# A block ahead of the barrier, evictions with the norm's factor, and head-norm matmuls between pairs of k tiles in a two-layer hybrid decoder step

## The chip, the cores and the metric

The kernel runs on one core of a Trainium2 chip. The time is device time of one execution in microseconds (us), lower is better. Before the change it is 3043.86 us, the median of three runs (3041.05 to 3045.55).

## The reference

One step of a two-layer decoder for 256 prompt tokens and 8 sample tokens (264 columns), all in fp32. Per layer:

```
xn = rmsnorm(x, norm_mix);  proj = xn @ w_in        # 2048 -> u, q, k, v, qi, ki, wi, gates
q = rope(rmsnorm(q, q_norm)); k = rope(rmsnorm(k, k_norm)); qi, ki = rope(qi), rope(ki)
y_att = sparse attention: an indexer (qi, ki, wi) picks keys (top 64 prompt, top 256 sample)
y_ssm = S5 scan of u (state 64 groups x 64), gelu, gated by w_glu
x = x + (sig(g0) * (y_ssm @ w_branch0) + sig(g1) * (y_att @ w_branch1)) @ w_out
x = x + (silu(hn @ w_gate) * (hn @ w_up)) @ w_down,  hn = rmsnorm(x, norm_ffn)
```

The outputs are x, the new keys, values and indexer keys of each layer, and the last states of the scan. `rmsnorm(x, g)` is x times g times one factor per token, 1/sqrt(mean(x^2) + eps); the head norm is the same over the 128 entries of a head.

## The kernel before

Activations lie transposed: 128 features on the partitions, the 264 tokens as columns; x has 16 such slices (k tiles). Weights stream through a ring of six slots of 512 KB, one *unit* (128 outputs, 8 k tiles) in each; two units make a block f (units 2f and 2f+1) and one output slice. SyncE loads unit u once unit u-6 is done (semaphore `units`). A block accumulates in one of four PSUM banks (`main[f % 4]`), and whoever evicts it frees the bank (`bank_free`).

A matmul is either *plain* (fp32, raw weights; each shows as two records) or *split*: ScalarE casts the weights to their high part (L1051, `highs_to`), VectorE subtracts to get the low part (L1355, `lows_to`), the activations are split likewise (x_high by ScalarE at L1088, x_low by VectorE at L1362), and three one-pass matmuls (L624, L625, L626) replace one plain product (L628). Units 2 to 9 (blocks 1 to 4) are plain; from unit 10 on they are split, apart from some later ones. `SPLIT` lists them, and TensorE waits before each split unit for its low part. All engines run their streams in the order written.

**Start of a layer.** The layers are separated by a barrier of all engines; ahead of the first one stands a prologue that loads x, squares it, and scales it by the gains (xg). After it, in each layer, TensorE sums the squares over the partitions with a matmul by ones (L655); ScalarE takes the root (L1082), VectorE the reciprocal (L1358), and makes the 16 slices xn = xg times factor (L1365), then the 16 x_low. Blocks 1 and 2 take xg, so that their results are multiplied by the factor as VectorE evicts them (L1370); blocks 3 and 4 take xn and ScalarE evicts them (L1061). VectorE then makes the S5 angles (L1376 to L1390), a chain of 15 small operations (L1394 to L1408), three wide ones (L1413 to L1415), the lows of units 10 and 11, three wide ones (L1417 to L1419), the lows of units 12 and 13, powers (L1431 to L1436), the lows of units 14 and 15. ScalarE has an Exp (L1090), which needs a table load, right after the x_high.

In layer 0 the end of the FFN's last phase makes xg for layer 1 (L1847) and adds the squares (L1856), and SyncE loads units 2 to 7 of layer 1 at L543.

**Head norm.** ScalarE squares a head slice (L1179, two buffers), TensorE adds it over its partitions into row t of one bank (L817: weights 128 rows by 12 columns) for 12 heads; ScalarE takes the root (L1193), VectorE the reciprocal (L1645), and TensorE spreads row t over 128 partitions (L833: weights 12 rows by 128 columns) into one of four banks, from which VectorE scales the head (L1653). Between these stand `fill(n)`, n whole w_in units of 24 split matmuls: unit 93 after the first `spread_rows` (L808, part of the sample key selection, 128x128), 94 after the second, 95 after head sum 8, 96 and 97 after the last sum, 98 after spread 5 and 99 after the last. Then follows `s5_out(0)` (L769). `LATE` gives which of four places holds the high part of units 92 to 105; places 2 and 3 lie on data of the key selection, so ScalarE waits for its end (`gix_ready`) before it writes them.

**End.** x is stored in four parts of four slices (528 KB), each when its last slice is final (L571).

Of the kernel before, what the change touches and what calls it, by code (L numbers as in the profile page):

```python
# [51 lines left out]
LATE = {92: 0, 93: 1, 94: 0, 95: 1, 96: 2, 97: 3, 98: 0, 99: 2, 100: 3, 101: 0, 102: 2, 103: 3, 104: 0, 105: 2}  # L52
# [64 lines left out]
def build(nc, d, o):  # L117
    with ExitStack() as ctx:
# [295 lines left out]
        qroped = sem("qroped")  # L414
        vt_ready, v_copied, kvn_ready, kvn_copied = sem("vt_ready"), sem("v_copied"), sem("kvn_ready"), sem("kvn_copied")
# [25 lines left out]

        with nc.Block() as block:
            @block.sync
            def _(sp):
                for p in range(4):
                    sp.dma_start(x[:, 4 * p:4 * p + 4, :], d["x"][:, 4 * p:4 * p + 4, :]).then_inc(x_part[p], 16)
                sp.dma_start(consts[:, 0:4 * P], d["consts"][:, 0:4 * P]).then_inc(consts_in, 16)
                for u in range(2, 4):
                    sp.dma_start(ring[:, u, :], d["w_in"][0, u - 2]).then_inc(u_in[u], 16)
                sp.dma_start(consts[:, 4 * P:NCONST], d["consts"][:, 4 * P:NCONST]).then_inc(consts_rest, 16)  # L450
                for u in range(4, 8):
                    sp.dma_start(ring[:, u % 6, :], d["w_in"][0, u - 2]).then_inc(u_in[u % 6], 16)

            @block.scalar
            def _(act):
                act.dma_start(gn[:], d["gn"][0]).then_inc(gn_in, 16)
                act.dma_start(tables, d["tables"]).then_inc(tables_in, 16)
                for p in range(4):
                    act.wait_ge(x_part[p], 16)
                    nc.scalar.activation(first_sq[:, 4 * p:4 * p + 4, :], x[:, 4 * p:4 * p + 4, :], ACT.Square).then_inc(sq_ready, 1)  # L460
                    if p >= 2:
                        act.wait_ge(gn_in, 16)
                        for k in range(4 + 2 * p, 6 + 2 * p):
                            nc.scalar.activation(xg[:, k, :], x[:, k, :], ACT.Copy, scale=gn[:, 0, k:k + 1])

                act.wait_ge(sq_ready, 4)
                nc.scalar.activation(small[:, 6:7], first_sq[:, 0, 0:1], ACT.Sqrt)

            @block.vector
            def _(dve):  # L470
                v = nc.vector
                tt, tsc = v.tensor_tensor, v.tensor_scalar
                v.memset(small[:, 7:8], EPS)

                def add_part(p):
                    dve.wait_ge(sq_ready, p + 1)
                    if p >= 2:
                        dve.wait_ge(sq_added, p - 1)
                    tt(acc, first_sq[:, 0:4, :] if p == 1 else acc, first_sq[:, 4 * p:4 * p + 4, :], ALU.add).then_inc(sq_added, 1)

                dve.wait_ge(gn_in, 16)
                for p in (0, 1, 3):
                    dve.wait_ge(x_part[p], 16)
                    for k in range(4 * p, 4 * p + 4):
                        tsc(xg[:, k, :], x[:, k, :], gn[:, 0, k:k + 1], None, ALU.mult)
# [28 lines left out]
        for layer in range(DEPTH):  # L514
            with nc.Block() as block:
# [11 lines left out]
                def _(sp):  # L527
# [45 lines left out]
                    for up, count, cols, half, n0, _ in PHASES:  # L573
# [8 lines left out]
                        if not up and half == 1:  # L582
# [14 lines left out]
                    if layer == DEPTH - 1:  # L597
                        sp.wait_ge(x_out, 64 * DEPTH)
# [3 lines left out]
                def _(pe):  # L602
                    mm = nc.tensor.matmul

                    def unit_part(u, seq, c, full, high, low, k0, n, opens, closes, made=None):
# [23 lines left out]
                        if k0 + n == 8:  # L629
                            m.then_inc(units, 1)  # L630
# [4 lines left out]
                    def w_in_unit(f, c, made=None):  # L635
                        unit_part(2 * f + c, f, c, xg if f < 3 else xn, xh, xl, 0, 8, c == 0, c == 1, made)
# [10 lines left out]
                    def x_made(k):  # L647
                        pe.wait_ge(xn_ready, k + 1)

# [153 lines left out]
                    def spread_rows(h):  # L803
# [6 lines left out]
                        fill(1)  # L810

                    def sum_heads(first, last):
                        for t in range(first, last + 1):
                            if t == 0:
# [3 lines left out]
                               start=t == 0, stop=t == NHK - 1).then_inc(qsum_ready, 1)  # L818

# [3 lines left out]
                    sum_heads(6, 8)  # L823
                    fill(1)
                    sum_heads(9, NHK - 1)
                    fill(2)
                    pe.wait_ge(spread_used, 6)
                    for t in range(NHK):
# [6 lines left out]
                        if t in (5, NHK - 1):  # L835
                            fill(1)
# [184 lines left out]
                    for up, count, cols, half, n0, seq0 in PHASES:  # L1021
                        if up:
                            split_blocks(seq0, n0, 2 * HF, 2, 8, xfh, xfl, None if half else x_scaled)
                        else:
                            split_blocks(seq0, n0, NT, 2, 11, hdh, hdl, hidden(half))

                @block.scalar
                def _(act):
# [67 lines left out]
                    for f in range(3, 10):  # L1096
                        evac_one(f)
                    act.drain()
                    act.wait_ge(bank_free[1], 4)
                    act.wait_ge(bank_free[2], 3)  # L1100
# [73 lines left out]
                    for t in range(NHK):  # L1174
# [10 lines left out]
                        if t == 10:  # L1185
                            act.wait_ge(gix_ready, 1)
                            highs_to(96)
                        if t == 11:
                            highs_to(97)
                            evac_gates(47, 1)  # L1190
# [3 lines left out]
                    highs_to(98)  # L1194
# [143 lines left out]
                def _(dve):  # L1338
# [25 lines left out]
                    for k in range(NT):  # L1364
                        tt(xn[:, k, :], xg[:, k, :], rs[:, 0, :], ALU.mult).then_inc(xn_ready, 1)  # L1365
                    for k in range(NT):
                        split_low(k)
                    for f in range(1, 3):
                        dve.wait_ge(units, 2 * f + 2)
                        tt(proj[:, f, :], main[f][:, 0:T], rs[:, 0, :], ALU.mult).then_inc(bank_free[f], 1)  # L1370
# [20 lines left out]
                    lows_to(8)  # L1391
# [147 lines left out]
                    def pick():  # L1539
# [24 lines left out]
                        lows_to(93)  # L1564
                        for h in range(2):
                            if h == 1:
                                lows_to(94)
# [12 lines left out]
                        lows_to(97)  # L1580
# [66 lines left out]
                    lows_to(98)  # L1647
                    for t in range(12):
                        if t == 6:
                            lows_to(99)  # L1650
# [163 lines left out]
                    def finish(i, s, up, half, n0, seq0):  # L1814
# [22 lines left out]
                        if not up and s % 2 == 1:  # L1837
# [7 lines left out]
                            if half == 1 and layer < DEPTH - 1:  # L1845
                                k = 4 * i + m
                                tsc(xg[:, k, :], x[:, k, :], gn[:, 0, k:k + 1], None, ALU.mult)  # L1847
# [217 lines left out]
```

## Time and profile before

| | us |
|---|---|
| median of three runs | 3043.86 |
| profiled execution | 3041.63 |
| its span | 3039.8 |
| VectorE busy in the span | 1965.2 (65%) |
| ScalarE busy | 1247.8 (41%) |
| first matmul of layer 0 | 14.81 after the span's start |
| last matmul before layer 1's barrier ends | 1522.12 |
| last VectorE operation of the program ends | 3035.62 |
| first of x loads issued in the prologue | 0.74 |

The profile names engines PE (TensorE), PEld (its weight loads), DVE (VectorE), ACT (ScalarE), POOL (GpSimd) and SP (SyncE). A share of busy time is an average; what a change is worth is read at the place where TensorE waits. Ends of matmuls are modelled, so paces are taken from one start to the next.

### The profile page before, as it was taken

Reading aid. Unit: us, or ns where it says so; the run is one execution under the profiler, and the core shown is the slowest. Engines: PE = TensorE matmul, PEld = TensorE weight load, DVE = VectorE, ACT = ScalarE, POOL = GpSimd, SP = SyncE. Lnnn points to the kernel's source line nnn. Section 1 sums busy time; section 2 is a strip of 40 time slices with the busy share of each in tenths; the row PEclk is TensorE's granted clock in tenths of the full one; section 3 lists DMA queues with packets and bytes.
Section 4 is the critical chain, followed back from the end, with each engine's and each line's share of the span. In section 5 each row is a group of like instructions: output and inputs, shape, how many; then the busy total and the mean of one; then the engine's idle time right before and its main releaser. Section 6 shows DMA issues by size and latency. Waiting matters only on the chain. (4 is left out here: it accounts for less than half of the span.)

```text
span 3039.8 us, 58606 instructions
## 1 busy us (share of the span) xinstructions
PE 2994.0 (98%) x23480; PEld 2852.2 (94%) x23480; DVE 1965.2 (65%) x3141; ACT 1247.8 (41%) x1767; POOL 253.3 (8%) x239
## 2 busy tenths in 40 slices
PE   8999999999999999999999999999999999999999
PEld 7988888999999999999988888889999999999999
DVE  7559888577655545555575697885776565455653
ACT  4443333544554333334344422344445443333332
POOL 4320000400000000000043200013000000000000
PEclk9999999999999999999999999999999999999999
DMA  7547444745655655556555473447556555555564
GB/s 253 164 145 203 145 141 145 243 167 178 196 185 182 199 172 174 185 181 206 187 194 167 149 204 126 143 163 230 170 177 199 182 183 198 167 181 181 185 205 135
DMA packets 150191, 546.45 MB, mean 180 GB/s; under 512 B 19824, under 2 KB 25072, under 8 KB 149520
## 3 DMA queue, kind: packets, MB, share of 16 engines
q1 hardware_dynamic: 137296, 507.40, 50.0%
q0 software_dynamic: 12096, 35.67, 4.6%
q8 instruction: 112, 1.84, 0.3%
q10 hardware_dynamic: 640, 1.16, 0.1%
q14 instruction: 47, 0.39, 0.0%
HBM read 536.95 MB, written 7.21 MB: 179 GB/s over the span
## 5 line engine op out<-in xcount | busy, mean ns | idle before, releaser
L1790 DVE TENSOR_TENSOR w_ffn_low<-ring_ffn,w_ffn_high 128x1024 fp32r<-128x1024 f32 (+1 forms) x480 | 638.8, 1332 | 456.0 <-ACT w_ffn_high L1300 456.0
L1300 ACT ACTIVATE w_ffn_high<-ring_ffn 128x1024 fp32r<-128x1024 f32 (+1 forms) x480 | 547.9, 1142 | 641.8 <-PE main L1013 640.9
L1011 PE MATMUL main<-x_ffn_high,w_ffn_high 128*128 128x264 f32 x2816 | 792.1, 281 | 0.0
L1013 PE MATMUL main<-x_ffn_high,w_ffn_low 128*128 128x264 f32 x2816 | 791.7, 281 | 0.0
L1012 PE MATMUL main<-x_ffn_low,w_ffn_high 128*128 128x264 f32 x2816 | 791.7, 281 | 0.0
L1011 PEld LDWEIGHTS main<-x_ffn_high,w_ffn_high 128*128 128x128 f32 x2816 | 526.8, 187 | 0.1
L1012 PEld LDWEIGHTS main<-x_ffn_low,w_ffn_high 128*128 128x128 f32 x2816 | 526.8, 187 | 0.1
L1013 PEld LDWEIGHTS main<-x_ffn_high,w_ffn_low 128*128 128x128 f32 x2816 | 526.8, 187 | 0.0
L1013 PE MATMUL main<-hidden_high,w_ffn_low 128*128 128x264 f32 x1408 | 395.8, 281 | 0.0
L1011 PE MATMUL main<-hidden_high,w_ffn_high 128*128 128x264 f32 x1408 | 395.8, 281 | 0.0
L1012 PE MATMUL main<-hidden_low,w_ffn_high 128*128 128x264 f32 x1408 | 395.8, 281 | 0.0
L628 PE MATMUL main<-xn,ring 128*128 128x264 f32 x1632 | 377.6, 388 | 0.0
L628 PEld LDWEIGHTS main<-xn,ring 128*128 128x128 f32 x1632 | 305.4, 190 | 49.9 <-issue 0.8
L626 PE MATMUL main<-x_high,w_low 128*128 128x264 f32 x1200 | 342.0, 285 | 0.0
L1011 PEld LDWEIGHTS main<-hidden_high,w_ffn_high 128*128 128x128 f32 x1408 | 263.4, 187 | 0.0
L1012 PEld LDWEIGHTS main<-hidden_low,w_ffn_high 128*128 128x128 f32 x1408 | 263.4, 187 | 0.0
L1013 PEld LDWEIGHTS main<-hidden_high,w_ffn_low 128*128 128x128 f32 x1408 | 263.4, 187 | 0.0
L624 PE MATMUL main<-x_high,w_in_high 128*128 128x264 f32 x880 | 259.4, 295 | 3.4 <-DVE w_low L1355 3.1
L625 PE MATMUL main<-x_low,w_in_high 128*128 128x264 f32 x880 | 250.1, 284 | 0.0
L626 PEld LDWEIGHTS main<-x_high,w_low 128*128 128x128 f32 x1200 | 227.4, 190 | 0.0
L1051 ACT ACTIVATE w_mid_high<-ring 128x1024 fp32r<-128x1024 f32 x144 | 151.5, 1055 | 144.4 <-PE main L626 144.4
L1355 DVE TENSOR_TENSOR w_low<-ring,w_mid_high 128x1024 fp32r<-128x1024 f32 x144 | 175.5, 1224 | 52.8 <-ACT w_mid_high L1051 51.1
(373 smaller groups left out, 4767.7 us busy)
## 6 DMA issues: line engine op xcount, KB each, us to landing
ring_ffn<-in_w_up SPq DMA_DIRECT2D x352, 512.0 KB, 3.2
ring<-in_w_in SPq DMA_DIRECT2D x260, 512.0 KB, 3.4
ring_ffn<-in_w_down SPq DMA_DIRECT2D x128, 704.0 KB, 4.1
ring<-in_w_br SPq DMA_DIRECT2D x64, 512.0 KB, 3.9
ring<-in_w_out SPq DMA_DIRECT2D x64, 512.0 KB, 3.1
w_low<-in_w_in POOLq DMA_DIRECT2D x20, 512.0 KB, 6.9
ring<-in_w_glu SPq DMA_DIRECT2D x16, 512.0 KB, 3.7
out_x<-x SPq DMA_DIRECT2D x8, 528.0 KB, 5.9
```

The source lines that it names most:

```text
L624: mm(out, weight(wh, u, k), high[:, kk, :], start=starts, stop=False)
L625: mm(out, weight(wh, u, k), low[:, kk, :], start=False, stop=False)
L626: m = mm(out, weight(wl, u, k), high[:, kk, :], start=False, stop=stops)
L628: m = mm(out, weight(raw, u, k), full[:, kk, :], start=starts, stop=stops)
L1011: mm(out, wfh[:, slot, w], high[:, kk, :], start=kk == 0, stop=False)
L1012: mm(out, wfh[:, slot, w], low[:, kk, :], start=False, stop=False)
L1013: m = mm(out, wfl[:, slot, w], high[:, kk, :], start=False, stop=kk == chunks * kts - 1)
L1051: af(high, raw, ACT.Copy).then_inc(unit_high, 1)
L1300: af(wfh[:, s, 0:cols], ring_ffn[:, s, 0:cols], ACT.Copy).then_inc(high_ready, 1)
L1355: tt(low, raw, high.bitcast(F32), ALU.subtract).then_inc(unit_low, 1)
L1790: tt(wfl[:, s, 0:cols], ring_ffn[:, s, 0:cols], wfh[:, s, 0:cols].bitcast(F32), ALU.subtract).then_inc(low_ready, 1)
```

## The change

1. Block 2 (units 4 and 5) is computed ahead of the barrier, from xg: in the prologue for layer 0, at the end of layer 0 for layer 1 (`first_block`). Its weights are loaded ahead of the other units. After the barrier TensorE does L655, block 1, then 3 and 4. `units` is raised by three when unit 3 is done.
2. Blocks 3 and 4 take xg too, and VectorE evicts all four with the factor (`gather_block`). The xn and x_low operations alternate. The casts of units 10 and 11 move ahead of ScalarE's Exp, the lows of both behind the angles.
3. Each of the 12 head sums and 12 spreads is followed by two k tiles of w_in (6 split matmuls, `pair`), with one whole unit between sums and spreads. `LATE` and the places of casts and lows of units 94 to 99 follow.
4. At the end of layer 1, slices 12 to 15 of x are stored one by one.

```diff
+        def first_block(pe, layer, gained):
+            for u in (4, 5):
+                pe.wait_ge(u_in[u], 16 * (G_END // 6 * layer + 1))
+                for k in range(8):
+                    kk = 8 * (u - 4) + k
+                    gained(kk)
+                    nc.tensor.matmul(main[2][:, 0:T], ring[:, u, k * P:(k + 1) * P], xg[:, kk, :], start=kk == 0, stop=kk == NT - 1)
@@ prologue, sync: x parts 0, 1, unit 4, x parts 2, 3, consts, units 5, 2, 3, consts, units 6, 7
+            @block.tensor
+            def _(pe):
+                def gained(k):
+                    if 8 <= k < 12:
+                        pe.wait_ge(x_gained_act, k - 7)
+                    else:
+                        pe.wait_ge(x_gained, k + 1 if k < 8 else k - 3)
+                first_block(pe, 0, gained)
@@ layer, sync, end
-                                for u in range(2, 8):
+                                for u in (4, 5, 2, 3, 6, 7):
                                     prefetch(u)
-                            store_x(3)
+                            if layer < DEPTH - 1:
+                                store_x(3)
+                                continue
+                            for k in range(12, NT):
+                                sp.wait_ge(resid, 2 * NT + k + 1)
+                                sp.dma_start(o["x"][:, k, :], x[:, k, :]).then_inc(x_out, 16)
@@ layer, tensor
-                            m.then_inc(units, 1)
+                            m.then_inc(units, 3 if u == 3 else 1)
-                        unit_part(2 * f + c, f, c, xg if f < 3 else xn, ...)
+                        unit_part(2 * f + c, f, c, xg if f < 5 else xn, ...)
-                    w_in_blocks(1, 2)
-                    for c in range(2):
-                        w_in_unit(3, c, x_made)
-                    w_in_blocks(4, 1)
+                    w_in_blocks(1, 1)
+                    w_in_blocks(3, 2)
@@ head norm, tensor
-                        fill(1)
+                    def pair(n):
+                        nonlocal filled
+                        w_in_piece(filled // 2, filled % 2 * 8 + n % 4 * 2, 2)
+                        filled += n % 4 == 3
@@ in sum_heads, after the matmul of head t
+                            pair(t)
                     spread_rows(0)
                     sum_heads(0, 5)
                     spread_rows(1)
-                    sum_heads(6, 8)
+                    sum_heads(6, NHK - 1)
                     fill(1)
-                    sum_heads(9, NHK - 1)
-                    fill(2)
@@ in the spreads, after the matmul of head t
-                        if t in (5, NHK - 1):
-                            fill(1)
+                        pair(t)
@@ layer 0, tensor, after the last FFN phase
+                    if layer < DEPTH - 1:
+                        pe.wait_ge(bank_free[2], (SEQ_UP + 4 * HF + 2 * NT) // 4 + 1)
+                        first_block(pe, layer + 1, lambda k: pe.wait_ge(x_gained, k + 1))
@@ scalar
                         af(xh[:, k, :], xn[:, k, :], ACT.Copy).then_inc(xh_ready, 1)
+                    highs_to(11)
                     act.wait_ge(params_in, 80)
                     af(disc[:, 0, :], ssmp[:, 2, :], ACT.Exp).then_inc(trig_ready, 1)
@@ vector, start of a layer
+                    def gather_block(f):
                         dve.wait_ge(units, 2 * f + 2)
-                        tt(proj[:, f, :], main[f][:, 0:T], rs[:, 0, :], ALU.mult).then_inc(bank_free[f], 1)
+                        tt(proj[:, f, :], main[f % 4][:, 0:T], rs[:, 0, :], ALU.mult).then_inc(bank_free[f % 4], 1)
+                    for k in range(NT + 2):
+                        if k < NT:
+                            tt(xn[:, k, :], xg[:, k, :], rs[:, 0, :], ALU.mult).then_inc(xn_ready, 1)
+                        if k >= 2:
+                            split_low(k - 2)
+                    for f in range(1, 4):
+                        gather_block(f)
@@ vector, after the angles
-                    lows_to(8)
+                    lows_to(11)
+                    gather_block(4)
                     dve.wait_ge(trig_ready, 4)
```

## Rows read from the trace of the kernel before

**Rows 1.** The page: busy time, share, count of each engine.
```profile
PE 2994.0 (98%) x23480; PEld 2852.2 (94%) x23480; DVE 1965.2 (65%) x3141; ACT 1247.8 (41%) x1767; POOL 253.3 (8%) x239
```

**Rows 2.** Timeline of TensorE at layer starts: start, length, instruction, count [idle before, releaser].
```profile
46.25 0.48 PE L624 MATMUL main<-x_high,w_in_high 128*128 128x264 f32 x1
...
1525.53 1.22 PE L655 MATMUL side<-rs,consts 128*128 128x264 f32 x2 [3.41 <-PEq L1943]
...
1555.96 0.48 PE L624 MATMUL main<-x_high,w_in_high 128*128 128x264 f32 x1
```

**Rows 3.** Busy time by stage: PE, PEld, DVE, ACT, POOL; PEclk, DMA, GB/s.
```profile
14.80:20.00 5.20, 5.19 (x12) 4.07 (x13) 3.39 (x6) 1.60 (x5) 0.07 (x1) 1.00 1.05 392
20.20:32.00 11.80, 11.80 (x55) 10.08 (x54) 9.66 (x29) 5.78 (x15) 8.91 (x2) 1.00 0.58 202
1887.20:1890.60 3.40, 3.40 (x18) 3.40 (x17) 1.01 (x1) 0.00 (x0) 0.00 (x0) 0.50 0.00 0
```

**Rows 4.** Timeline of VectorE across the start of layer 1.
```profile
1523.02 0.96 DVE L1856 TENSOR_TENSOR rs<-rs,tmp 128x264 f32<-128x264 f32 x2
...
1529.14 5.59 DVE L1365 TENSOR_TENSOR xn<-arena,rs 128x264 f32<-128x264 f32 x16
...
1542.12 0.43 DVE L1370 TENSOR_TENSOR proj<-main,rs 128x264 f32<-128x264 f32 x1 [1.54 <-PE main L628]
...
1545.02 0.19 DVE L1394 TENSOR_TENSOR apow<-proj 128x32 f32<-128x32 f32 x1 [0.41 <-ACT proj L1095]
...
1552.22 2.36 DVE L1355 TENSOR_TENSOR w_low<-ring,w_in_high 128x1024 fp32r<-128x1024 f32 x2
...
1558.37 2.40 DVE L1355 TENSOR_TENSOR w_low<-ring,w_in_high 128x1024 fp32r<-128x1024 f32 x2
...
1565.56 2.36 DVE L1355 TENSOR_TENSOR w_low<-ring,w_in_high 128x1024 fp32r<-128x1024 f32 x2
```

**Rows 5.** Timeline of ScalarE at the start of layer 1.
```profile
1535.20 1.28 ACT L1090 ACT_TABLE_LOAD   x1
...
1544.90 1.04 ACT L1051 ACTIVATE w_in_high<-ring 128x1024 fp32r<-128x1024 f32 x1
```

**Rows 6.** Timeline of TensorE where the kind of matmul changes, layer 0.
```profile
101.31 1.05 PE L682 MATMUL side<-proj,consts 128*128 128x264 f32 x4
...
102.32 0.28 PE L625 MATMUL main<-x_low,w_in_high 128*128 128x264 f32 x1
...
361.12 0.28 PE L626 MATMUL main<-x_high,w_low 128*128 128x264 f32 x1
361.32 1.74 PE L817 MATMUL side<-tmp,rs 128*12 128x264 f32 x6
363.00 0.39 PE L624 MATMUL main<-x_high,w_in_high_v 128*128 128x264 f32 x1
363.22 0.28 PE L625 MATMUL main<-x_low,w_in_high_v 128*128 128x264 f32 x1
...
373.83 2.93 PE L833 MATMUL side<-rs,consts 12*128 12x264 f32 x12
376.70 0.39 PE L624 MATMUL main<-x_high,w_in_high_b 128*128 128x264 f32 x1
```

**Rows 7.** DMA issues: the first 4 us (ring), and the last store; KB each, us to landing.
```profile
ring<-in_w_in SPq DMA_DIRECT2D x2, 512.0 KB, 8.1
...
out_x<-x SPq DMA_DIRECT2D x1, 528.0 KB, 2.7
```

**Rows 8.** Timelines of TensorE and VectorE in the head norm's stretch.
```profile
348.47 1.91 PE L808 MATMUL side<-proj 128*128 128x390 f32 x6
...
385.77 3.84 PE L769 MATMUL side<-arena,cc 128*32 128x264 f32 x64
...
1866.24 2.02 PE L808 MATMUL side<-proj 128*128 128x390 f32 x6
...
1870.84 1.23 DVE L1355 TENSOR_TENSOR w_low<-ring,w_in_high_v 128x1024 fp32r<-128x1024 f32 x1
```

More of the change, by code:

```diff
@@ L414, in build @@
         qroped = sem("qroped")
+        x_gained, x_gained_act = sem("x_gained"), sem("x_gained_by_act")
         vt_ready, v_copied, kvn_ready, kvn_copied = sem("vt_ready"), sem("v_copied"), sem("kvn_ready"), sem("kvn_copied")
@@ L444, in _, with load_x, load @@
             def _(sp):
-                for p in range(4):
+                def load_x(p):
                     sp.dma_start(x[:, 4 * p:4 * p + 4, :], d["x"][:, 4 * p:4 * p + 4, :]).then_inc(x_part[p], 16)
+                def load(u):
+                    sp.dma_start(ring[:, u % 6, :], d["w_in"][0, u - 2]).then_inc(u_in[u % 6], 16)
+                load_x(0)
+                load_x(1)
+                load(4)
+                load_x(2)
+                load_x(3)
                 sp.dma_start(consts[:, 0:4 * P], d["consts"][:, 0:4 * P]).then_inc(consts_in, 16)
-                for u in range(2, 4):
-                    sp.dma_start(ring[:, u, :], d["w_in"][0, u - 2]).then_inc(u_in[u], 16)
+                for u in (5, 2, 3):
+                    load(u)
                 sp.dma_start(consts[:, 4 * P:NCONST], d["consts"][:, 4 * P:NCONST]).then_inc(consts_rest, 16)
-                for u in range(4, 8):
-                    sp.dma_start(ring[:, u % 6, :], d["w_in"][0, u - 2]).then_inc(u_in[u % 6], 16)
+                for u in (6, 7):
+                    load(u)
+            @block.tensor
[6 more added lines that the diff above has]
+                first_block(pe, 0, gained)
             @block.scalar
@@ L597, in _ @@
                     if layer == DEPTH - 1:
-                        sp.wait_ge(x_out, 64 * DEPTH)
+                        sp.wait_ge(x_out, 64 * DEPTH + 48)
                     sp.wait_ge(stored, 48)
@@ L635, in w_in_unit @@
                     def w_in_unit(f, c, made=None):
-                        unit_part(2 * f + c, f, c, xg if f < 3 else xn, xh, xl, 0, 8, c == 0, c == 1, made)
+                        unit_part(2 * f + c, f, c, xg if f < 5 else xn, xh, xl, 0, 8, c == 0, c == 1, made)
                     def w_in_blocks(first, count):
@@ L1095, in _ @@
                     af(disc[:, 5, :], disc[:, 6, :], ACT.Sin).then_inc(trig_ready, 1)
-                    for f in range(3, 10):
+                    for f in range(5, 10):
                         evac_one(f)
                     act.drain()
-                    act.wait_ge(bank_free[1], 4)
-                    act.wait_ge(bank_free[2], 3)
+                    for bank in range(4):
+                        act.wait_ge(bank_free[bank], 4 if bank < 2 else 3)
                     act.sem_inc(proj_copied, 10)
@@ L1193, in _ @@
                     af(rs[0:NHK, 0, :], side[0][0:NHK, 0:T], ACT.Sqrt, bias=small[0:NHK, 7:8], scale=1.0 / HD).then_inc(qstd_ready, 1)
-                    highs_to(98)
+                    highs_to(97)
+                    evac_gates(47, 1)
+                    act.wait_ge(gix_ready, 1)
                     highs_to(99)
@@ L1579, in pick @@
                         dve.sem_inc(gix_ready, 1)
-                        lows_to(97)
+                        lows_to(96)
                     def scan(half, between=None):
@@ L1645, in _ @@
                     v.reciprocal(rs[0:NHK, 0, :], rs[0:NHK, 0, :]).then_inc(qinv_ready, 1)
-                    lows_to(98)
+                    lows_to(97)
                     for t in range(12):
-                        if t == 6:
-                            lows_to(99)
+                        if t in (2, 6):
+                            lows_to(98 + t // 6)
                         dve.wait_ge(qinv_spread, t + 1)
```

25 lines of the change are left out of this document (6 added, 19 removed).

## The prediction

> **What bounds the kernel now.** I read the page's busy times first: TensorE is busy for 98% of the span [rows 1]. So only three things move the time: its remaining idle, work whose pace is below the full one, and anything new that keeps it waiting. The waits view gives 18.2 us of TensorE's idle to the two layer starts (14.8 and 3.4), and about 1 us at a time elsewhere. The timeline of TensorE then shows where each layer's first split block starts [rows 2]; the table by stage shows its pace [rows 3]; the timelines of VectorE and ScalarE show who feeds it there [rows 4, 5]; and the single rows around the small matmuls show what a change from one kind of matmul to another costs [rows 6].
>
> Paces that I use. A plain fp32 product is two records of 0.222 us at full speed (55 records touch 11.8 us), so a w_in block of 16 products takes 7.1 us; at the start of the run the step is 0.44 (12 records in 5.2 us) although that stretch's granted clock is noted as 1.00, and TensorE had been idle before it [rows 3]. A split k tile is three records of about 0.121, so a pair of k tiles is 0.73 us, a unit 2.9 and a block 5.9.
>
> **Part 1, the block ahead and the four evictions with the norm's factor.** Call L the start of the matmul at L655, the first work of a layer. The new block now stands ahead of the barrier, so the barrier waits for it. In layer 1 its weights are issued at 1510 and its last input is scaled at 1523.1, just after the last FFN matmul ends (1525.53 less 3.41 idle is 1522.1) [rows 2]. It runs 1522.1 to 1529.3. Before, VectorE's last add ended at 1523.98 and L655 came 1.55 us later [rows 2, 4]; with that same distance L becomes 1530.8, 5.3 later than 1525.53. In layer 0 the unit of weights that stood sixth, after 2.4 MB, landed 8.1 us after its issue at 3.4, thus at 11.5 [rows 7]; at the implied 1.3 us for each transfer, the one that now stands third (the block's first unit) lands at about 7.4, and the one that stands seventh (its second unit) where the seventh landed before, 8.1 after 3.9: 12.0. TensorE starts at 7.4 with 12 records at 0.44, then 20 at 0.222: it ends at 17.1, L is 18.7 instead of 14.8. If it is at full speed sooner, the second unit's landing still bounds it: 12.0 plus 3.6 plus 1.5 is 17.1.
>
> From L on TensorE has L655 and three plain blocks (0.5 and 21.4): block 5, the first split one, can start at L+21.9 and end at L+27.7. Before it started at 46.25 and 1555.96 [rows 2], so by TensorE alone 5.7 and 3.3 us would be won.
>
> VectorE's chain hangs on L, and it is nearly gapless already: its idle between 1529 and 1559 is 1.54 and 0.41 [rows 4]. Step by step: the factor is there and xn begins at L+3.0 (1525.53 to 1529.14, less 0.6 that L655 lost to the slow clock); 32 operations of xn and x_low, now alternating, 11.2: L+14.2. Three evictions of 0.44, the third not before its block ends at L+14.7: L+15.6. ScalarE has its sixteenth x_high at about L+14.0; then, new and ahead of the Exp, the two casts of units 10 and 11 at 1.04 each, then the table load of 1.28 [rows 5]: Exp ends at L+17.7. Before, this load lay under x_low; now VectorE waits about 2 us for it. Its angle operations (1542.55 to 1544.6) end at L+19.9, the lows of units 10 and 11 at L+22.2, in time for block 5. Then the fourth eviction, 0.4; then what the change leaves between lows 11 and 12: the chain from 1545.02 to 1552.22, 7.2, which used to stand ahead of low 10, and three wide operations, 3.8; low 12 ends at L+34.8. Block 5 ends at L+27.7. **TensorE waits 7 us for low 12 in each layer.** Block 6 then starts at 53.5 instead of 52.1, and at 1565.6 instead of 1561.8. Low 14 comes 7.2 after low 12 (1558.37 to 1565.56) [rows 4] while block 6 lasts 5.9, another 1.3; the slow clock that a 7 us stop should bring costs about the same and lies beside this wait, 0.1 more. Layer 0 loses 2.8, layer 1 loses 5.2: **8.0**. Units 16 on find VectorE caught up. The weight loads of units 10 and 11 are issued at L+7.6 together with 9 and are back before ScalarE's casts at L+14; sample keys on GpSimd's queue are asked for no later. Bounds: layer 0 from -0.1 (L at 17.1) to +3.5, layer 1 from +3.7 (no low 14 wait) to +6.
>
> **Part 2, the head norm's sums and spreads.** The rows show three cases [rows 6]. A group with 128 rows and 128 columns, L682, costs nothing extra: from its first record to the second of the following split is 1.01, that is 4 times 0.222 and 0.12. L817, 128 rows by 12 columns: 0.20 from the last split record to it instead of 0.12; its six records take 1.68 instead of 1.34; and the first step of the split after it is 0.22 instead of 0.12. L833, 12 rows by 128 columns and no square to wait for: its 12 records take 2.87 instead of 2.67; with the same 0.09 ahead and 0.10 behind, a round trip costs 0.39. Of L817's 0.34 in the middle I give 0.11 to the way out, as half of L833's 0.20, and 0.23 to the one wait for ScalarE's square that falls among three heads (two buffers): a round trip costs 0.30. I take 0.30 and 0.39, since they are the same instructions on both sides of the passage; the other end is L682's nothing.
>
> The Trainium skill, TensorEngine Tiling (Array Packing), section Key Properties, says that changing the tiling mode, not just the tile, drains the engine; TensorE: Matmul & The Clock Gate gives a drain as some 0.175 us. By that estimate two passages cost 0.35 per head; the sum would be 0.1 us higher. It is a rule against this change, and these rows bear it out, L682's exemption too.
>
> Before, a layer made 5 such round trips; changed, it makes 24. The changed stretch from the first L808 to L769: two groups L808 at 1.6 (1.91 with the last record's modelled end), 12 heads at 0.445+0.73+0.30=1.47, one unit 2.9, 12 spreads at 0.445+0.73+0.39=1.56: 42.4. New in it is a wait: low 95 stands behind two groups of the second spread on VectorE, ending 5.9 after that L808 begins (1866.24 to 1870.84 and 1.23) [rows 8], while the pair of head 8 wants it at 5.1: 0.7. So 43.1 against 385.77-348.47=37.3 in layer 0 [rows 8]: +5.8. In layer 1 two stretches of 3.4 us at half clock follow the two L833 groups (one shown) [rows 3]; the units in them take 1.5 longer each, which alternating work should spare: 43.1 against 40.4, +2.7. Together **+8.5**. The square waits are in this. ScalarE's root and VectorE's reciprocal lie beside the one unit between sums and spreads (2.9, with the root no longer behind a Tanh eviction); without that cover 0.5 each. Bounds: no passage cost, 24 heads at 1.17, is 34.1, plus a longer low 95 wait 1.4: -1.8 and -4.9; above, both spreads partly at half clock, +5.
>
> **Part 3, last slices singly.** The last store moves 132 KB instead of 528 KB, of a landing of 2.7 [rows 7]; at the same rate of some 400 KB per us 1.0 less. The three earlier singles lie under the last matmuls; the last wait counts all. -1.0, bounds -1.3 and 0.
>
> Sum: 8.0+8.5-1.0=+15.5. The profiled execution took 3041.6, thus 3057.1; the three timed runs have a median 2.2 higher, and against 3043.9 it is 3059.4. I say 3059. What the measurement can tell from no change is about 0.2%, 6 us.
>
> **The rivals.**
> - B, passages are free when a head stands alone between pairs, its weights loaded under the split matmuls that run. For it: L682 [rows 6]. Against: both odd shapes pay on both sides. (The Trainium skill, TensorE: Matmul & The Clock Gate, section Part 2, has weight loads pulled ahead of matmuls in flight; that alone would give this 3044.) Heads -6.7 in all, total +0.3: 3044, no change. It decides by one price: at 48 round trips the kernel is slower by over 0.2% from about 0.13 each, and not slower below 0.01.
> - C, VectorE keeps up at the layer starts, since alternating xn with x_low frees ScalarE earlier. Then the 5.7 and 3.3 are won: -9.0+8.5-1.0, 3042. Against: the 12.6 us on VectorE between lows 11 and 12 are in program order, against 5.9 of block 5.
> - D, B and C both: 3027.
> - E, the alternating stretches hold TensorE at half clock at times, as after the L833 groups before. For it: 12-row work half the time. A third of the two spread stretches at half speed costs some 6: 3065.
>
> Chances: forecast 0.60, B 0.13, C 0.10, D 0.04, E 0.13. The forecast and E are slower, with a small part of B and C: slower 0.76; same 0.16; faster 0.08. Range 3043 to 3066: it holds half of C and most of B, and the upper bounds short of their sum.
>
> **What would show it.** In the changed profile: the 16 products of the block end at about 17 and 1529, L655 starts at about 18.7 and 1530.8; TensorE's waits name the low of w_in (L1355's successor) with about 7 us before block 6 in each layer and 1 before block 7; one step of a pair loop is 1.47 (sums) and 1.56 (spreads); the stretch from first L808 to L769 is 43 in both layers, with no half clock in layer 1. The prediction is wrong if low 12 comes before L+28, or if the pair loop steps at 1.2.

## The result, and the profile after

The changed kernel takes 3060.5 us (median of 5 runs, 3059.8 to 3061.2), the kernel before 3044.8 beside it (5 runs, 3041.1 to 3045.6): a ratio of 1.0056, interval 1.0046 to 1.0067, or 15.7 us slower. The forecast was 3059. A second comparison on another chip gave the same: 3060.1 against 3043.9, 1.0056 (1.0043 to 1.007). Of all executions of the kernels below one stands apart: one of the 12 of e3_full took 5113.1 us, at a mean granted clock of 0.643, and its ratio leaves it out.

The page first. It hardly tells the two kernels apart: TensorE has as many instructions as in [rows 1] and 11.6 us more busy time. A *passage* is the change from one shape of matmul to another, on the way in or out. Work that passages or a slow clock stretch counts as busy; only the rest of the 19.6 us by which the span grew, 8.0, is idle.

```profile
PE 3005.6 (98%) x23480; PEld 2850.8 (93%) x23480; DVE 1967.2 (64%) x3145; ACT 1249.0 (41%) x1763; POOL 247.5 (8%) x239
```

Next the view of waits for TensorE, which says what it waited for: us in total, times, longest.

```profile
PE main L658 <- DVE w_low L1388: 19.6, 9, 7.7
PE main L450 <- DVE arena L514: 7.5, 1, 7.5
...
PE side L957 <- DMA bbt<-in_ck,gix: 2.7, 2, 1.7
PE side L686 <- PEq L1979: 1.5, 1, 1.5
PE side L686 <- PEq L541: 1.5, 1, 1.5
```

The lows of w_in (L1388, before L1355) lead it, with 7.7 as the longest. Where that falls stands in TensorE's timeline; its rows answer to [rows 2]. L450 is the block ahead, L686 was L655, L658 was L624.

```profile
7.51 8.96 PE L450 MATMUL main<-arena,ring 128*128 128x264 f32 x32 [7.51 <-DVE arena L514]
18.01 0.69 PE L686 MATMUL side<-rs,consts 128*128 128x264 f32 x2 [1.54 <-PEq L541]
...
39.70 0.48 PE L658 MATMUL main<-x_high,w_in_high 128*128 128x264 f32 x1
52.97 0.56 PE L658 MATMUL main<-x_high,w_in_high 128*128 128x264 f32 x1 [7.08 <-DVE w_low L1388]
61.37 0.28 PE L658 MATMUL main<-x_high,w_in_high 128*128 128x264 f32 x1
...
1531.78 7.28 PE L450 MATMUL main<-arena,ring 128*128 128x264 f32 x32
1540.60 0.68 PE L686 MATMUL side<-rs,consts 128*128 128x264 f32 x2 [1.54 <-PEq L1979]
...
1562.94 0.36 PE L658 MATMUL main<-x_high,w_in_high 128*128 128x264 f32 x1 [0.30 <-issue]
1576.69 0.56 PE L658 MATMUL main<-x_high,w_in_high 128*128 128x264 f32 x1 [7.67 <-DVE w_low L1388]
```

The reader is to see block 5 start 6.5 us sooner than before in layer 0 (39.70 against 46.25), and block 6 then stand still for 7.1 and 7.7 us. Block 7 starts at 61.37, so block 6 lasted 8.4 us where a block at full speed lasts 5.8. The windows say why, and give the head norm's stretches (first L837, which was L808, to first L798, which was L769). Columns as in [rows 3]; the figure behind the five busy times, 0.51 in the first row, is the granted clock.

```profile
48.50:58.70 10.20, 5.73 (x27) 5.76 (x28) 9.40 (x23) 0.02 (x1) 0.00 (x0) 0.51 0.05 17
1574.20:1581.00 6.80, 4.31 (x20) 4.34 (x21) 6.21 (x17) 0.00 (x0) 0.00 (x0) 0.51 0.00 0
351.79:395.21 43.42, 43.06 (x231) 28.50 (x229) 24.57 (x45) 15.40 (x24) 0.00 (x0) 1.00 0.26 85
1874.86:1918.28 43.42, 43.05 (x231) 28.50 (x229) 24.55 (x45) 15.40 (x24) 0.00 (x0) 1.00 0.26 85
```

The head norm's stretches of the kernel before, the same view:

```profile
348.47:385.77 37.30, 37.03 (x230) 28.70 (x228) 25.14 (x45) 14.94 (x24) 0.00 (x0) 1.00 0.30 99
1858.24:1898.61 40.37, 40.10 (x231) 31.77 (x229) 25.15 (x45) 14.94 (x24) 0.00 (x0) 0.92 0.28 92
```

During the stop the granted clock falls to one half (1.2 GHz instead of 2.4) and stays there into block 6. The head norm takes 43.4 us in both layers, with no slow clock in it, against 37.3 and 40.4 before. One step of its sums, in TensorE's timeline (answers to [rows 6]; a step is from one L850 to the next: 1.47):

```profile
353.64 0.62 PE L850 MATMUL side<-tmp,rs 128*12 128x264 f32 x2
...
355.11 0.62 PE L850 MATMUL side<-tmp,rs 128*12 128x264 f32 x2
...
356.58 0.62 PE L850 MATMUL side<-tmp,rs 128*12 128x264 f32 x2
```

VectorE in layer 1 (answers to [rows 4]): the wait for the Exp behind the casts, lows 10 and 11, the fourth eviction L1399, the chain from L1432, and only then lows 12 and 13.

```profile
1559.41 0.19 DVE L1413 TENSOR_TENSOR proj<-proj 128x32 f32<-128x32 f32 x1 [3.42 <-ACT proj L1125]
...
1561.62 2.35 DVE L1388 TENSOR_TENSOR w_low<-ring,w_in_high 128x1024 fp32r<-128x1024 f32 x2
1563.89 0.42 DVE L1399 TENSOR_TENSOR proj<-main,rs 128x264 f32<-128x264 f32 x1
1564.23 0.18 DVE L1432 TENSOR_TENSOR apow<-proj 128x32 f32<-128x32 f32 x1
...
1575.32 2.36 DVE L1388 TENSOR_TENSOR w_low<-ring,w_in_high 128x1024 fp32r<-128x1024 f32 x2
```

ScalarE there (answers to [rows 5]): both casts waited for their weights, 0.63 and 0.43 us.

```profile
1554.81 1.06 ACT L1085 ACTIVATE w_in_high<-ring 128x1024 fp32r<-128x1024 f32 x1 [0.63 <-DMA ring<-in_w_in]
...
1556.30 1.06 ACT L1085 ACTIVATE w_in_high<-ring 128x1024 fp32r<-128x1024 f32 x1 [0.43 <-DMA ring<-in_w_in]
```

And the last store (answers to [rows 7]), 132 KB, landed 1.8 us after its issue instead of 2.7:

```profile
out_x<-x SPq DMA_DIRECT2D x1, 132.0 KB, 1.8
```

Between the two profiled executions the time went to: layer starts +3.3 (the transposes L700 at 78.85 against 75.58) and +6.8 (1601.96 against 1585.31 is 16.7, less the 9.8 gathered by the end of layer 0); head norm +6.1 and +3.0; tail -0.9; that is 18.3 of the 19.6 by which the span grew. The remaining 1.3 are about what the longer wait for the key gather makes: 2.7 above, and in TensorE's waits of before

```profile
PE side L926 <- DMA bbt<-in_ck,gix: 1.3, 2, 0.8
```

The medians differ by less, 15.7, because the profiled execution of before was one of its fastest. The mean granted clock of each execution shows what sets them apart. Of the 38 of before on the two chips used last below, those with a clock of 0.998, as the profiled one had, took 3040.7 to 3043.5 us, and those with 0.996 or 0.997 took 3043.6 to 3046.0. So the kernel before loses more to half clock in most of its executions than its trace shows.

### The profile page after: what moved, and what is told of

Its sections match the earlier page's. It is cut to its first block and busy times, and to the rows that moved or that the text cites. A ratio compares the mean times of both kernels' runs of the same rounds, so it can differ in the third digit from the quotient of the medians.

```text
span 3059.4 us, 58609 instructions
## 1 busy us (share of the span) xinstructions
PE 3005.6 (98%) x23480; PEld 2850.8 (93%) x23480; DVE 1967.2 (64%) x3145; ACT 1249.0 (41%) x1763; POOL 247.5 (8%) x239
## 5 line engine op out<-in xcount | busy, mean ns | idle before, releaser
L662 PE MATMUL main<-xn,ring 128*128 128x264 f32 x1504 | 348.8, 388 | 0.0
L662 PEld LDWEIGHTS main<-xn,ring 128*128 128x128 f32 x1504 | 280.9, 190 | 45.9 <-issue 0.8
L658 PE MATMUL main<-x_high,w_in_high 128*128 128x264 f32 x880 | 261.5, 297 | 18.4 <-DVE w_low L1388 17.9
L1388 DVE TENSOR_TENSOR w_low<-ring,w_mid_high 128x1024 fp32r<-128x1024 f32 x144 | 175.6, 1225 | 52.6 <-ACT w_mid_high L1085 50.9
```

Of the source, the lines that this page charges most:

```text
L658: mm(out, weight(wh, u, k), high[:, kk, :], start=starts, stop=False)
L662: m = mm(out, weight(raw, u, k), full[:, kk, :], start=starts, stop=stops)
L1388: tt(low, raw, high.bitcast(F32), ALU.subtract).then_inc(unit_low, 1)
```

## The experiments

All times are medians, each ratio is to the kernel before on the same chip (before: 3055.8 for the first four, where its runs spread over 3050 to 3059; 3043.9 for the next four; 3044.0 for the last four). "Stretch" is the head norm's, in us, in layers 0 and 1. The changed kernel itself was not run on the chip of the first four.

| kernel | us | ratio (interval) | stretch L0, L1 |
|---|---|---|---|
| e1_fills | 3061.6 | 1.0020 (1.0011 to 1.0029) | 41.9, 40.4 |
| e2_pairs | 3060.1 | 1.0013 (1.0004 to 1.0022) | 43.4, 43.4 |
| e3_full | 3055.7 | 1.0001 (0.9992 to 1.001) | 36.0, 36.0 |
| e4_lows | 3067.5 | 1.0038 (1.0025 to 1.005) | 43.4, 43.4 |
| e5_after | 3060.1 | 1.0056 (1.0043 to 1.007) | 43.4, 43.4 |
| e6_pairs_full | 3035.9 | 0.9975 (0.9965 to 0.9985) | 36.0, 36.0 |
| e7_jit | 3042.0 | 0.9995 (0.9985 to 1.0004) | 43.4, 43.4 |
| e8_jit_full | 3027.7 | 0.9946 (0.9933 to 0.996) | 36.0, 36.0 |
| e9_sums_full | 3037.6 | 0.9980 (0.9971 to 0.9989) | 40.7, 40.7 |
| e10_before_full | 3036.2 | 0.9973 (0.9963 to 0.9983) | 36.0, 36.0 |
| e11_fills_full | 3028.8 | 0.9949 (0.9935 to 0.9962) | 36.0, 36.0 |
| e12_loads | 3060.1 | 1.0051 (1.0037 to 1.0065) | 43.4, 43.4 |

**The parts by themselves.** e1_fills is the changed kernel with part 2 taken back:

```diff
-                            pair(t)
...
-                    sum_heads(6, NHK - 1)
+                    sum_heads(6, 8)
                     fill(1)
+                    sum_heads(9, NHK - 1)
+                    fill(2)
```

> The changed kernel with the head norm's part as it was before (whole units between groups of heads, the old places of the high parts). My account: the layer starts cost 3.3 and 6.8 us there and the last store gains 0.95, so this kernel stands 9 us above the kernel before (about 3054) and 9 below the changed one's profile; the stretch from the first L808-kind matmul to s5_out is back to 37.3 us in layer 0. Rival (the pairs are the only cost, the layer starts break even): within 1 us of the kernel before. Rival (the two parts amplify each other): under 6 us above it.

e2_pairs is the kernel before with part 2 alone:

```diff
                                start=t == 0, stop=t == NHK - 1).then_inc(qsum_ready, 1)
+                            pair(t)
```

> The kernel before with the head norm's part of the change alone. My account: +6.1 us in layer 0's stretch and +3.1 in layer 1's, 9 us in all, about 3054. The stretch is 43.4 us in both layers, with steps of 1.47 and 1.57 us per head. In an execution of the kernel before that has more or fewer half-clock stretches behind the spreads, the difference is up to 3 us smaller or larger. Rival (a single head between pairs costs nothing extra): no slower than before. The sum of this difference and of the first kernel's should be the whole change's, within 1 us, if the parts are independent.

Measured: +5.8 and +4.3 us, where about 9 was expected of each. The signs are as expected, the sizes smaller, and the two add up to 10.1, not to the whole change's 15.7: as a test that the parts are independent this failed. e2's stretches are 43.4 in both layers, the same as in the changed kernel, so the mechanism is there. No trace of before was taken on that chip, but the mean granted clocks of the executions point at what hides it: 0.995 is the median of before's 28 (0.994 to 0.997), 0.998 that of e2's 11 (0.997 to 0.999). Over 3055 us this difference is an estimated 9 us of clock that e2 gets back, against 6.1 in each layer that its stretches lose; 3 us are left, and 4.3 were measured. The clocks are rounded, so this is a rough account. For e1, whose clock is 0.994, this doesn't help, and the missing 3 us stay open. e1's stretch in layer 0 was expected at 37.3 and is 41.9, because half clock stands in it, now in both layers, behind each group of 12-row spreads (windows of e1; the clock is 0.50 and 0.52):

```profile
383.00:389.80 6.80, 6.80 (x28) 5.89 (x27) 2.18 (x4) 0.00 (x0) 0.00 (x0) 0.50 0.03 13
1908.80:1912.20 3.40, 3.40 (x17) 3.40 (x17) 0.74 (x1) 0.00 (x0) 0.00 (x0) 0.52 0.00 0
```

**What a passage costs.** e3_full is the changed kernel with both odd shapes filled up to 128 by 128 (the one-hot table widened to match):

```diff
-mm(side[0][0:NHK, 0:T], one_hot[:, NHK - 1 - t:2 * NHK - 1 - t], sq[:, t % 2, :],
+mm(side[0][:, 0:T], one_hot[:, NHK - 1 - t:NHK - 1 - t + P], sq[:, t % 2, :],
...
-mm(side[t % 4][:, 0:T], ident[0:NHK, t:t + 1].to_broadcast([NHK, P]), rs[0:NHK, 0, :],
+mm(side[t % 4][:, 0:T], ident[:, t:t + 1].to_broadcast([P, P]), rs[:, 0, :],
```

> The changed kernel with both kinds of head norm matmuls in the full 128x128 shape: the sums' weights have 128 columns (12 of use, the rest zeros), the spreads take all 128 rows (the identity's column t, zero outside row t). Same number of matmuls and of columns streamed. My account (the price is the passage between shapes, 0.30 and 0.39 us per round trip): steps of 1.17 and 1.17 us, 24 steps per layer, 8 us less per layer less about 1 us for a longer wait for low 95 and 0.5 for the reciprocal: 13 us less than the changed kernel, about 3047. Rival (the price is in switching between fp32 and one-pass products, or in the semaphore wait of each head): no change against the changed kernel.

Measured: level with before on that chip, and each stretch 36.0 instead of 43.4, so 14.8 us less in the two layers. The changed kernel wasn't timed there, so the expected 13 us can't be read off the time; the pair e7_jit and e8_jit_full below, on one chip, differs by the same edit, and by 14.3. The same matmuls with the same waits and kinds of product, more rows and columns of them, and 7.4 us less per layer: what is paid for is the change of shape. e9_sums_full (from e7 below) fills up only the sums:

> The changed kernel with the lows in time and the 12 sums as 128 by 128 matmuls, the 12 spreads still with 12 rows. The passages cost 0.30 per head for the sums and 0.39 for the spreads by the rows of before, so a step of the sums goes from 1.47 to 1.17 and one of the spreads stays at 1.57: the stretch from the first sum of squares to the score rows is 39.6 to 39.9 us, 3.6 less than with both odd shapes in each layer, and the time lies 6 to 7 under the kernel with the lows alone and 7 to 8 above the one with both. Rival: only the change between the two odd kinds counts, or one of them is free: steps of 1.17 or 1.57 in both.

Its steps are 1.18 for the sums and 1.57 for the spreads; the two windows of e7 and e9 in layer 0:

```profile
344.52:387.94 43.42, 43.06 (x231) 28.49 (x229) 24.54 (x45) 15.40 (x24) 0.00 (x0) 1.00 0.25 85
```

```profile
343.31:384.05 40.74, 39.67 (x231) 31.31 (x229) 24.58 (x45) 15.37 (x24) 0.00 (x0) 1.00 0.27 91
```

So a round trip costs 1.47-1.18=0.29 at 128 by 12 and 1.57-1.17=0.40 at 12 by 128 (1.17 is the spread's step in e8); I had read 0.30 and 0.39 off [rows 6]. The stretch came to 40.7, not 39.6 to 39.9: faster steps bring TensorE to low 95 sooner, and it waits 1.06 there instead of 0.36, in e9 as in e8, whose row this is. The time came to 3037.6; set beside e7 and e8 by the ratios, that is 4 to 5 under the one and 10 above the other, where 6 to 7 and 7 to 8 were expected.

```profile
358.26 0.39 PE L658 MATMUL main<-x_high,w_in_high_v 128*128 128x264 f32 x1 [1.06 <-DVE w_low L1388]
```

Both odd kinds pay, each by itself: the rival that one of them is free falls, and rival B with it. The Trainium skill, TensorEngine Tiling (Array Packing), section Key Properties, has a drain at each change of tiling mode, and by TensorE: Matmul & The Clock Gate, section Single matmul latency, two drains are an estimated 0.35. The two prices here, 0.29 and 0.40, lie on either side of that. No run here shows whether a drain is what is paid.

**What the alternation is worth without its passages.** e6_pairs_full is before with the pairs and the full shapes, e10_before_full before with the full shapes alone, still in groups between whole units.

> The kernel before with the pairs of part 2, and sums and spreads as 128 rows by 128 columns. Passage theory: both stretches take 36.0 us, as in the run of the changed kernel with full shapes, against 37.3 and 40.4 before, and no stretch at half clock follows a group of spreads: 5.7 us faster than the kernel before, a ratio of 0.998; 7.4 per layer less than the pairs alone. Rival, the alternation costs by itself or the half clock comes from elsewhere: stretches of 38 or more in one layer, time within 2 us of before.

> The kernel before with nothing changed but the shape of sums and spreads, 128 by 128; they still stand in groups between whole units. If the work with 12 rows is what brings half clock behind the groups of spreads, no half clock stands in either stretch and both last the same, 35 to 36 us: 37.3 and 40.4 less five round trips of 0.3 to 0.6, less 3.1 in layer 1; 6 us less than before in all. If the gap-free packing of single products brings it, layer 1 keeps its 3.4 us stretches at half clock. Pairs give nothing then: the same as the pairs with full shapes within 2 us.

They are 8.0 and 7.9 us faster than before: the pairs add nothing. Some 6 was expected of each, and the stretches give 5.6; the rest fits the clock of the executions, 0.999 or 1.000 in theirs and 0.996 to 0.998 in before's. Windows of e10, both stretches:

```profile
348.69:384.72 36.03, 35.76 (x230) 31.26 (x229) 25.14 (x45) 14.94 (x24) 0.00 (x0) 1.00 0.30 103
1857.29:1893.32 36.03, 35.76 (x231) 31.27 (x229) 25.14 (x45) 14.94 (x24) 0.00 (x0) 1.00 0.29 103
```

Against before's 37.3 and 40.4, layer 0 loses 1.3 for the five round trips (1.7 by the prices above: a group of three sums still takes 1.48 instead of the bare 1.34) and layer 1 besides them 3 us of half clock: the clock is 1.00 through both. With 128 rows no stretch of groups has half clock (e10 and e11, four stretches); with 12 rows three of four have it (e1 both, before layer 1), but not before's layer 0, at 1.00 from end to end. So the 12-row groups are needed for it here and don't always bring it; what decides is open, and whether the sums' shape has a part in it too, since e10 changes both. That the stretch is 36.0 in both arrangements, though one waits for low 95 and the other is taken to wait for squares, I didn't trace further.

**The layer starts.** The theory: low 12 comes late since 11 us of other work stand ahead of it in VectorE's program. e4_lows moves the lows forward:

```diff
                     gather_block(4)
+                    lows_to(13)
...
-                    lows_to(11)
+                    lows_to(15)
...
-                    lows_to(13)
+                    lows_to(17)
```

> The changed kernel with VectorE's lows of units 12 and 13 right behind the fourth eviction, 14 and 15 between the two groups of three wide operations, 16 and 17 after them. My account (TensorE waits 7 us for low 12 only because 11 us of other VectorE work stand ahead of it): low 12 is done at L+24 and 14 at L+33, block 6 starts at once at L+27.7, no half clock behind the wait; layer 0 gains 7.1 plus 2.6 of slow clock, layer 1 7.7 plus 1.9: 18 to 19 us less than the changed kernel, about 3042. Rival (VectorE's total work ahead is the bound, and the wait only moves to block 7 or to the transposes that need bbar): under 8 us less.

This failed: 11.7 us slower than before on that chip, where the expected 3042 would have been some 2 us faster. Block 6 did start at once, 46.98, but the stop came back at low 18, which now stood behind all the powers:

```profile
71.47 0.56 PE L658 MATMUL main<-x_high,w_in_high 128*128 128x264 f32 x1 [6.12 <-DVE w_low L1388]
```

The transposes stayed at 78.8. Two readings were left: VectorE has too much work up to there (then no order helps), or the order was wrong once more. The window from L (the layer's first matmul, L686) to the transposes (L700) speaks for the order, for VectorE (the third busy figure) is busy 51.2 of 59.5 us, e4's row:

```profile
19.25:78.78 59.53, 53.28 (x338) 49.49 (x339) 51.23 (x122) 25.00 (x40) 30.71 (x20) 0.94 0.61 212
```

e7_jit is e4 with the later lows put where TensorE comes to want them, beside e5_after, the changed kernel again on the same chip:

```diff
                         n *= 2
+                        if n == 4:
+                            lows_to(18)
                         if n == 8:
-                            lows_to(15)
+                            lows_to(19)
-                    lows_to(16)
+                    lows_to(20)
```

> The changed kernel once more, as the measure for the three beside it on the same chip. By the medians of the first comparison it is 15.7 us slower than the kernel before; the runs of the parts on the second chip (+5.8 without the pairs, +4.3 with the pairs alone) let me expect only 9 to 16 there. Its stretch from the first sum of squares to the score rows is 43.4 us in both layers, the transposes start near 78.9.

> The changed kernel with VectorE's lows where TensorE wants them: units 12 and 13 behind the fourth eviction, 14 and 15 between the two groups of wide operations, 16 and 17 behind them, 18 after the second and 19 after the third doubling of the powers, 20 behind the powers. Order theory (VectorE has 9 us of idle time within the 60 us from L on, so it isn't its total work that bounds): TensorE waits under 1 us at block 6 and under 1 us for low 18, the transposes start at 71 to 72.5 instead of 78.9 in layer 0 and 6 to 7.5 earlier in layer 1, in all 12 to 15 us less than the changed kernel run beside it. Total-work theory: the wait moves on once more, to low 19 or 20, the transposes stay at 78.8, within 2 us of the changed kernel.

Measured: e5_after 16.2 over before, just above the 9 to 16. e7_jit 3042.0 against 3060.1, 18 us less, the median 1.9 under that of before (which the interval doesn't tell apart). The same window in e7, and its row of the transposes (at 79.14 in e5_after):

```profile
19.52:71.64 52.12, 51.68 (x338) 47.90 (x339) 46.14 (x104) 25.15 (x40) 29.04 (x20) 1.00 0.70 242
```

```profile
71.64 1.04 PE L700 MATMUL side<-consts,proj 128*128 128x128 f32 x8
```

From L to the transposes 52.1 us instead of 59.9 in layer 0, and 51.8 instead of 60.9 in layer 1; TensorE's waits for lows in it fall to 0.3 and the clock stays at 1.00. The order was the bound, not the amount of work. Of the 18 us the two starts give 7.8 and 9.2. That is above my 12 to 15, as the slow clock went with the stop: e5 has 6.8 us of it in each start, e7 none in its whole trace.

e8_jit_full adds the full shapes, e11_fills_full is the same with the groups of before instead of pairs.

> The same with sums and spreads of the head norm as 128 by 128 matmuls. Order theory with the passage theory: 12 to 15 us at the layer starts and 2 times 7.4 us in the head norm, 27 to 30 us less than the changed kernel run beside it, which is 12 to 17 less than the kernel before. If the passages cost nothing of what I charge them: as the kernel with the order alone. Total-work theory: only the 14.8 of the head norm.

> Lows in time and full shapes as in the fastest kernel so far, but the head norm's work in groups between whole units as before. If alternation is worth nothing once its passages are gone, the time is that of the kernel with the pairs within 2 us and each stretch 35 to 36.5 us; if the groups still wait for ScalarE's squares and VectorE's reciprocal, each stretch is 1 us longer or more.

3027.7 and 3028.8: the fastest two, 16 and 15 us under before, e8 32 under the changed kernel, and once more the pairs are worth nothing that can be measured. e8's layer starts come 4.9 and 2.8 us sooner to the transposes than before's.

e12_loads, the changed kernel with

```diff
+                    for u in (10, 11):
+                        sp.dma_start(ring[:, u % 6, :], d["w_in"][layer, u - 2]).then_inc(u_in[u % 6], 16)
                     sp.dma_start(gqk[:], d["gqk"][layer]).then_inc(params_in, 16)
...
-                    for u in range(8, 12):
+                    for u in (8, 9):
```

> The changed kernel with the weights of units 10 and 11 asked for first behind the barrier (their buffers are free by the block ahead) instead of behind five parameter loads and units 8 and 9. In layer 1 of the changed kernel ScalarE waited 0.63 and 0.43 us for these two: with them early, low 12 comes 1.1 us sooner and block 6 starts at L+35.0 instead of L+36.1 in layer 1, nothing in layer 0; 1 us less in all, inside what the times can show. If parameters or units 8 and 9 come late instead, TensorE waits for the ring between L and L+20 and the time is longer.

Block 6 of layer 1 starts 35.1 after L (36.1 in the changed kernel), as expected; ScalarE's casts stand back to back. The time, 16.1 over before, doesn't tell it from the changed kernel.

```profile
1554.57 1.99 ACT L1087 ACTIVATE w_in_high<-ring 128x1024 fp32r<-128x1024 f32 x2
```

## Why the prediction was right, and where a term was off

- **L, the start of a layer's first matmul.** Forecast 18.7 and 1530.8; measured 18.01 in layer 0 (the block ahead ran from 7.51 to 16.47, not to 17.1), and in layer 1, less the 9.8 us gathered before it, 1530.8. The block comes ahead of the barrier as worked out. The same kernel's second trace, e5_after, has 19.26 (the block runs to 17.72), so 18.7 lies between two executions. What the reader shouldn't take from the waits view: its row names VectorE for the block's late start, in e7 and e8 it names the ring's load instead (7.7 and 7.3); the two come close together.
- **The stop at block 6.** Forecast 7 us, at 53.5 in layer 0; measured 7.08 at 52.97. Right in place, size and cause: e7 takes the cause away by order alone.
- **Layer starts, +2.8 and +5.2: mis-sized**, +3.3 and +6.8 measured. Two statements of the prediction failed. "The weight loads of units 10 and 11 ... are back before ScalarE's casts": not in layer 1, 1.06 us of waits. There the Exp came later too, VectorE waited 3.4 for it instead of about 2 (1.9 in layer 0), and low 12 ended at about L+36 instead of L+34.8; e12 gives 1.0 of it back. And the slow clock, which I laid beside the wait for low 14 at 0.1: low 14 was done at 59.9 (58.73 and 1.2) and 1583.7, and TensorE could have started some 0.2 later, the distance from low 12 to block 6; yet block 7 started at 61.37 and 1584.48, so the slow clock cost about 1.3 and 0.6 beyond that wait. Here a stop of 7 us on TensorE was paid twice: the stretch behind it at half clock was a second price.
- **Head norm, +5.8 and +2.7:** measured +6.1 and +3.0, stretch 43.4 against a forecast of 43.1. Steps 1.47 and 1.57 against 1.47 and 1.56; the wait for low 95 was 0.36 against 0.7, which is less than forecast, but each of the two groups L837 took 1.85 up to the next matmul (351.79 to 353.64) against 1.6, which outweighs it. The half clock of layer 1 went, as said.
- **Tail, -1.0:** the last store's landing is 0.9 shorter. Its worth was too small for a run of its own and was read off the traces only.
- **Rivals.** B (free passages) fell with the steps of 1.47 and 1.57, and by its cause in e3 and e9. C (VectorE keeps up) fell as told, but as a kernel of its own it is real: with the lows in time, e7 reaches the transposes 3.9 and 2.8 us sooner than before, where C had 5.7 and 3.3. That e7's 3042.0 and e8's 3027.7 stand where C and D put the time is in part chance, since their starts gained less than that. E (half clock in the alternating stretches) fell: 1.00 in every pair stretch.
- **What my theory of the starts lacked:** I first took moving a few lows ahead for the cure (e4). Each low has its own due time on TensorE, some 2.9 us after the last, and one left behind a 7.6 us chain stops it as surely as the first.

By medians the forecast of +15.5 met +15.7, but the sum was made for the profiled execution, and there it was 19.6: the terms above came to 18.3, 2.8 more than forecast, and the rest was not in the sum. The medians meet because most executions of before are slower than its profiled one, by a clock that no term of the sum has. The mechanism was right; the closeness of the number is luck.

## What to carry to other kernels

A matmul with 12 rows or 12 columns between full ones paid on the way in and out here, 0.29 to 0.40 us a round trip. Interleaving such matmuls singly multiplied that price; filling them up to the neighbours' shape removed it at no cost, and then grouping or interleaving made no difference. When work is brought ahead on the bounding engine, write down for each later step the time at which it will want its operands, and check the feeding engine's program order against each of them, not only the first.

## What was not expected of the hardware

- Groups of six spreads (12 records) with 12 rows, between whole units, are followed by 3.4 to 6.8 us at a granted clock of 0.50 in three of four stretches (before in layer 1, e1 in both layers; not before in layer 0), although TensorE is busy all the time; the same groups with 128 rows are not in any of four (e10, e11), nor are the 12-row spreads when each stands between split matmuls (43.4 us at 1.00).
- The larger matmul is no longer than the small one: two records of a sum take 0.61 us at 128 by 128 (e9) and 0.62 at 128 by 12. Their ends are modelled; the steps, 1.18 against 1.47, say it by starts.
- The chips differ by more than the change: before had a median of 3055.8 on one and 3043.9 and 3044.0 on two others. Part of it is the clock: 0.995 in the median execution on the first, 0.997 on the others, an estimated 6 us. All four traces of the first have 3.4 us at half clock near 2100 us, and none of the other traces has any there. Times are compared on the same chip only, or by their ratios to before; the head norm's stretches agree between chips to 0.03 us.
